# A hybrid decoder layer on one core: the first channel group's projections per token block over four weight tiles, and the input's squares added on VectorE

## The chip, the cores and the metric

The kernel runs on one core of a Trainium2 chip. The metric is the device time of the whole launch in microseconds (us), as the median of several runs. Besides these, one execution was recorded by the hardware profiler; its rows are quoted below.

## What is computed

One layer on 2048 tokens of 1024 channels, in float32. The input is RMS-normalised and projected; the projection feeds two token mixers; their outputs go through one output projection; a squared-ReLU MLP follows. Phase A of the kernel, which the change is about, computes the lines up to the silu of `u`:

```python
h_in = rms_norm(x, pre_mix_norm_w)                 # x * rsqrt(mean(x*x) + EPS) * w
proj = jnp.einsum("bsd,de->bse", h_in, w_in)       # -> qk_raw, v, o, gates, conv_val, conv_gate
qk = silu(causal_depthwise_conv(qk_raw, qk_conv_w, qk_conv_b))        # width 4
u = conv_val * sigmoid(conv_gate)
u = causal_depthwise_conv(u, conv_w, conv_b)                          # width 31
y_conv = silu(layer_norm_per_group(u))                                # 4 groups of 128 channels
h_tilde = mlstm_chunkwise(q, k, v, i_pre, f_pre)                      # chunks of 128 tokens
y = concat([y_mlstm, y_conv]) @ w_out;  x = x + rms_norm(y)
x = x + rms_norm(relu(rms_norm(x) @ w_ff1)**2 @ w_ff2)
```

## The kernel before

**Phases.** Phase A makes the normalised input and all input projections and stores what the mixers need in DRAM. Phase B walks the 16 chunks of the mLSTM and makes the output projection. The MLP follows. Each float32 operand of a projection is split into a high and a low part, so every product of two tiles is three matmuls.

**Token blocks.** The 2048 tokens are four blocks (`tb`) of 512; a block has eight k-tiles (`kt`) of 128 channels. Per block: ScalarE squares the eight tiles (`square_x`, L378); GpSimd adds them in seven steps of 128x512 (L276) for blocks 1 to 3, while for block 0 TensorE itself sums the eight squares; a matmul with ones (`sum_squares`, L301, L305) sums over channels; ScalarE makes the reciprocal root in two activations (`rstd_x`, L386, L388); VectorE scales each tile (L558), ScalarE copies its high part (L394), VectorE subtracts for the low part (L553).

**Slots.** TensorE's work in phase A is a list of 100 slots, each one weight tile times one token block (24 matmuls of 128x512), or for `v` and `o` a pair of weight tiles times two chunks (48 of 128x256). Channel group g has the slots `gate` and `val` for each of the four blocks, then `qk` for two tiles j and four blocks. The order is group 0, group 1, eight `v` slots, group 2, eight `v`, group 3, four `gates`, sixteen `o`. Slot s writes PSUM bank s mod 6 and waits until slot s-6 has been evacuated: by VectorE for `val` (`glu`, L585, the gated product into `u_buf`), by ScalarE for all others. Every engine goes through `for s in range(N_SLOTS)` in program order, so one late instruction holds all that stand behind it on its engine. The matmul with ones for block tb+1 stands behind slots 0, 2 and 4.

**The wide convolution.** A unit u is one group and one half (1024 tokens), eight units in all. It has a first tap on ScalarE (`first_tap`, L445) and 30 taps on VectorE (`tap`, L597), each over 128x1024. `tap_plan()` fixes when it is built how many taps follow each slot: a slot gives room 100, a tap takes 26, half a qk convolution takes 78 (`convolve_qk`, L609: three steps of 128x1024). `CONV_END[u]` is the slot after whose taps unit u is complete. From it hang, by slots: +1 two sums by TensorE (which waits in its queue for tap 30(u+1)), +2 centring on VectorE (L635), +3 squaring on ScalarE, +4 again two sums by TensorE, +5 the reciprocal root on ScalarE (L501 to L506), +6 a multiply on GpSimd (L284), +7 silu and the store to `yc` on ScalarE (L510, L513). The code of the planner before gives `CONV_END` = 19, 28, 38, 46, 57, 65, 75, 85. A `u_buf` ring of three means that the `glu` that begins unit u waits for the taps of unit u-3, and the planner forces these to be placed before it.

**The end of phase A.** `TAIL_SLOT` is 94. ScalarE does the softplus of the gates in slot 94; behind slot 95 TensorE waits for the reciprocal root of all eight units, since these use the same PSUM banks, and then makes `carry_in`; `carry_out` and `columns` stand behind slots 96 and 97. GpSimd loads the gate rows and later stores the rows `neg_m` and `inter`. SyncE waits for every store of `qk` and `yc`, then loads chunks 0 and 1 (ten DMAs of 256 KB, L921 to L923) and their rows (four, L927). Phase B begins when chunk 0 is complete.

**Weights.** A weight tile is loaded into a ring of four, its high part made by ScalarE (L401), its low part by VectorE for tiles 0 to 3 (L568) and by GpSimd for the others (L259).

## Time and profile before

| what | value |
|---|---|
| median of 3 runs | 2191.96 us (2190.08 to 2196.56) |
| profiled execution, its own time | 2193.84 us |
| span of the profiled execution | 2192.0 us |
| TensorE, matmuls busy | 2108.2 us, 96% |
| VectorE busy | 1481.8 us, 68% |
| ScalarE busy | 892.9 us, 41% |
| GpSimd busy | 530.9 us, 24% |
| mean granted TensorE clock | 0.984 |

The span is from the first to the last instruction; 1.84 us of the profiled execution's time lie around it. The shares are averages over stages with different limits, so a stage is read from its own window. A matmul's busy time is that of one instruction, and neighbours overlap.

### The profile page before, as it was taken

To read this page: it belongs to the slowest core of one execution; us is meant where nothing else is said; L and a number is where in the kernel's file an instruction comes from. 1 tells how busy PE (TensorE), PEld (TensorE's weight loads), DVE (VectorE), ACT (ScalarE), POOL (GpSimd) and SP (SyncE) were. 2 spreads that over 40 slices of the span, in tenths; PEclk is the share of its full clock that TensorE was granted. 3 is DMA by queue.
4 is the path that set the end of the run, shared out by engine and by line. 5 is a ranking of instruction groups with operands and counts; after the bars stand their busy time and mean duration, and the time that the engine had idled before them with its cause. 6 is when DMAs were issued, how large, how long until landed. Compare 5 with 4: busy or idle time off the path is not lost. (4 is left out here: it accounts for less than half of the span.)

```text
span 2192.0 us, 27093 instructions
## 1 busy us (share of the span) xinstructions
PE 2108.2 (96%) x10177; PEld 1758.5 (80%) x10177; DVE 1481.8 (68%) x1922; ACT 892.9 (41%) x1504; POOL 530.9 (24%) x304
## 2 busy tenths in 40 slices
PE   5899999999998999979999989999999999999998
PEld 3588988987987888758888878888878888888886
DVE  6789999979336777776666776666745536544275
ACT  5432423324243544545454554444513313223153
POOL 4202102112110232143222232223172233500012
PEclk8999999999999999989999999999999999999999
DMA  5011212202264767554555655554666464543366
GB/s 193 20 58 39 83 44 66 80 20 71 66 227 152 237 229 244 182 177 156 159 159 159 217 181 159 159 159 155 222 248 232 154 246 149 198 173 135 135 240 211
DMA packets 253522, 339.19 MB, mean 155 GB/s; under 512 B 11537, under 2 KB 196113, under 8 KB 239569
## 3 DMA queue, kind: packets, MB, share of 16 engines
q1 hardware_dynamic: 219344, 316.29, 43.2%
q10 hardware_dynamic: 33728, 21.04, 3.1%
q8 instruction: 82, 1.34, 0.2%
q14 instruction: 48, 0.39, 0.1%
q0 software_dynamic: 320, 0.13, 0.0%
HBM read 226.14 MB, written 111.28 MB: 154 GB/s over the span
## 5 line engine op out<-in xcount | busy, mean ns | idle before, releaser
L1561 PE MATMUL psum<-x_hi,w_hi_P 128*128 128x512 f32 x896 | 353.2, 394 | 21.3 <-DVE x_lo L1508 21.3
L1561 PE MATMUL psum<-x_lo,w_hi_P 128*128 128x512 f32 x896 | 351.8, 393 | 0.0
L1561 PE MATMUL psum<-x_hi,w_lo_P 128*128 128x512 f32 x896 | 351.8, 393 | 0.0
L1763 PE MATMUL psum<-w_hi,hid_hi 128*128 128x512 f32 x896 | 348.7, 389 | 1.7 <-DVE hid_lo L1655 1.7
L597 DVE SCALAR_TENSOR_TENSOR c_buf<-u_buf,par_a,c_buf 128x1024 f32<-128x1024 f32 x240 | 342.8, 1430 | 8.5 <-ACT c_buf L445 1.3
L1763 PE MATMUL psum<-w_lo,hid_hi 128*128 128x512 f32 x896 | 348.6, 389 | 0.0
L1763 PE MATMUL psum<-w_hi,hid_lo 128*128 128x512 f32 x896 | 348.6, 389 | 0.0
L1655 DVE TENSOR_TENSOR hid_lo<-hid_raw,hid_hi 128x1024 fp32r<-128x1024 f32 x112 | 176.4, 1612 | 209.6 <-ACT hid_hi L1650 209.6
L1477 POOL TENSOR_TENSOR w_raw<-w_raw 128x512 f32<-128x512 f32 x128 | 181.8, 1442 | 406.0 <-DVE w_lo_P L1490 401.4
L1490 DVE TENSOR_TENSOR w_lo_P<-w_raw,w_hi_P 128x512 fp32r<-128x512 f32 x224 | 182.3, 826 | 107.9 <-ACT w_hi_P L1486 104.9
L1650 ACT ACTIVATE hid_hi<-hid_raw 128x1024 fp32r<-128x1024 f32 x112 | 112.9, 1051 | 348.7 <-DMA hid_raw<-scratch_hid 348.7
L1486 ACT ACTIVATE w_hi_P<-w_raw 128x512 fp32r<-128x512 f32 x224 | 137.0, 627 | 259.2 <-PE psum L1561 258.5
L1561 PEld LDWEIGHTS psum<-x_hi,w_hi_P 128*128 128x128 f32 x896 | 170.2, 190 | 60.7 <-issue 25.6
L1561 PEld LDWEIGHTS psum<-x_lo,w_hi_P 128*128 128x128 f32 x896 | 170.4, 190 | 35.5
L1561 PEld LDWEIGHTS psum<-x_hi,w_lo_P 128*128 128x128 f32 x896 | 170.2, 190 | 35.7
L1763 PEld LDWEIGHTS psum<-w_hi,hid_hi 128*128 128x128 f32 x896 | 168.2, 188 | 37.4 <-issue 2.5
L1763 PEld LDWEIGHTS psum<-w_hi,hid_lo 128*128 128x128 f32 x896 | 168.2, 188 | 34.9
L1763 PEld LDWEIGHTS psum<-w_lo,hid_hi 128*128 128x128 f32 x896 | 168.2, 188 | 34.8
L1611 POOL TENSOR_TENSOR w_raw<-w_raw,w_grain 128x1024 f32<-128x1024 f32 x48 | 139.1, 2912 | 224.9 <-DMA w_grain<-in_w 224.9
L259 POOL TENSOR_TENSOR w_lo<-w_raw,w_hi 128x1024 fp32r<-128x1024 f32 x21 | 56.8, 2715 | 332.6 <-ACT w_hi L401 332.6
L337 PE MATMUL psum<-big_hi,w_hi 128*128 128x512 f32 x272 | 114.4, 420 | 15.2 <-DVE big_lo L553 11.6
L337 PE MATMUL psum<-h_hi,w_hi 128*128 128x512 f32 x272 | 109.5, 402 | 7.2 <-ACT h_hi L394 4.0
(231 smaller groups left out, 3885.0 us busy)
## 6 DMA issues: line engine op xcount, KB each, us to landing
scratch_hid<-stage SPq DMA_DIRECT2D x224, 256.0 KB, 3.7
hid_raw<-scratch_hid SPq DMA_DIRECT2D x56, 1024.0 KB, 4.9
w_raw<-in_w SPq DMA_DIRECT2D x52, 1024.0 KB, 5.1
w_grain<-in_w SPq DMA_DIRECT2D x48, 512.0 KB, 5.1
x_raw<-scratch_h2s SPq DMA_DIRECT2D x14, 1024.0 KB, 7.6
w_raw<-in_w_in SPq DMA_DIRECT2D x25, 512.0 KB, 3.9
scratch_h2s<-h2s SPq DMA_DIRECT2D x8, 1280.0 KB, 9.3
scratch_qk<-qout ACTq DMA_DIRECT2D x16, 512.0 KB, 3.0
```

Of the source, the lines that this page charges most:

```text
L259: nc.gpsimd.tensor_tensor(w_lo[:, RING[t]], w_raw[:, RING[t]], w_hi[:, RING[t]].bitcast(F32), ALU.subtract).then_inc(sem["w_lo"], 1)
L337: mm = nc.tensor.matmul(out, a, b, start=kt == 0 and i == 0, stop=kt == KT - 1 and i == 2)
L597: nc.vector.scalar_tensor_tensor(out=out, in0=src, scalar=par[:, CONV_W + g * CW + k:CONV_W + g * CW + k + 1], in1=out, op0=ALU.mult, op1= ...
L1477: nc.gpsimd.tensor_tensor(raw_1(op), raw_1(a), raw_1(b), ALU.subtract).then_inc(sem["w1_t"], 1)
L1486: nc.scalar.activation(w1_hi[op][:], raw_1(op), ACT.Copy).then_inc(sem["w1_hi"], 1)
L1490: nc.vector.tensor_tensor(w1_lo[op][:], raw_1(op), w1_hi[op][:].bitcast(F32), ALU.subtract).then_inc(sem["w1_lo"], 1)
L1561: mm = nc.tensor.matmul(psum[:, bank_1(op, g), :], l, r, start=kt == 0 and i == 0, stop=kt == 3 and i == 2)
L1611: nc.gpsimd.tensor_tensor(part, part, grain[:, n % 2], alu).then_inc(sem["w2_t"], 1)
L1650: nc.scalar.activation(hid_hi[n % HID_RING][:, half_fps(h)], hid_raw[n % HID_RING][:, half_fps(h)], ACT.Copy).then_inc(sem["hid_hi"], 1)
L1655: nc.vector.tensor_tensor(hid_lo[n % HID_RING][:, half_fps(h)], hid_raw[n % HID_RING][:, half_fps(h)], hid_hi[n % HID_RING][:, half_fps(h) ...
L1763: mm = nc.tensor.matmul(psum[:, bank, :], l, r, start=f == 0 and k == 0, stop=f == NFP - 1 and k == 2)
```

## The change

Group 0 now runs block by block: slots 4tb to 4tb+3 are `qk` 0, `qk` 1, `gate` 0, `val` 0 of block tb, so all four first weight tiles are in use from the start. Tiles 2 and 3 are loaded ahead of blocks 2 and 3 of the input and are split behind block 0's normalisation. ScalarE's squares of a block fill all eight quarters of `c_buf` and of a part of `u_buf`, and VectorE adds them in three steps, 128x2048, 128x1024 and 128x512 (`add_squares`), behind the previous block's normalisation. Of block 0 VectorE makes the last four squares. The matmul with ones stands inside slots 2, 6 and 10, behind k-tile 3, 3 and 2. The evacuations of slots 0 to 9 are spread between the blocks. The half convolutions of `qk` 0 and 1 are placed at slots 13, 15, 17 and 19, in a second buffer for j = 1, and the planner gives room for taps only behind slot 13. Evaluated with the new lines, it gives 4 taps behind slot 15, then 1, 3, 1, 3, and 18 behind slot 20 (forced by the ring of `u_buf`), none behind 21 to 24, and `CONV_END` = 20, 36, 44, 54, 63, 71, 82, 90. GpSimd loads the gate rows in slot 90, and the rows have addresses of their own.

```diff
 def group_slots(g):
+    if g == 0:
+        for tb in range(NTB):
+            out += [("qk", 0, tb), ("qk", 1, tb), ("gate", 0, tb), ("val", 0, tb)]
+        return out
...
+def glu_end(u):
+
+    return SLOTS.index(("val", u // 2, 2 * (u % 2) + 1))
+
+
+FIRST_LOOP = 13
+Q_AT = {(j, half): {(0, 0): 13, (0, 1): 15, (1, 0): 17, (1, 1): 19}.get((j, half)) or SLOTS.index(("qk", j, 2 * half + 1))
+        for j in range(8) for half in range(2)}
+EARLY_EVACS = 10
+X_SUMS = {(2, 3): 1, (6, 3): 2, (10, 2): 3}
+
+
+def convs_at(s):
+    return [q for q in Q_AT if Q_AT[q] == s]
...
-        ready = DVE_TAPS * sum(SLOTS.index(("val", u // 2, 2 * (u % 2) + 1)) <= s for u in range(N_UNITS))
-        if s >= 2 * NTB:
-            room += 100 - 13 * (SLOTS[s][0] == "val")
-        if s and SLOTS[s - 1][0] == "qk" and SLOTS[s - 1][2] % 2 == 1:
-            room -= 78
+        ready = DVE_TAPS * sum(glu_end(u) <= s for u in range(N_UNITS))
+        if s > FIRST_LOOP:
+            room += 100 - 13 * (SLOTS[s][0] == "val") - 78 * len(convs_at(s - 1))
         more = max(0, min(ready - n, room // 26))
...
-FIRST_TAP = [max(min(s for s in range(N_SLOTS) if TAPS[s] > DVE_TAPS * u) - 1, glu_slot(u) + 2) for u in range(N_UNITS)]
+FIRST_TAP = [max(min(s for s in range(N_SLOTS) if TAPS[s] > DVE_TAPS * u) - 1, glu_end(u)) for u in range(N_UNITS)]
...
         def x_sq(n):
 
-            return c_buf[:, n % 4 // 2, n % 2 * TB:(n % 2 + 1) * TB]
-
-        def x_adds(n):
-
-            return (KT - 1) * (n // KT - 1) + max(n % KT, 1)
+            n %= KT
+            buf = c_buf[:, n // 2] if n < KT // 2 else u_buf[:, n // 2 - 1]
+            return buf[:, n % 2 * TB:(n % 2 + 1) * TB]
+
+        def x_squares(n):
+
+            return n + 1 - (KT // 2 if n >= KT // 2 else 0)
+
+        def x_total(tb):
+            return qout[:, (tb % 2) * TB:(tb % 2 + 1) * TB]
+
+        def qk_raw(j, half):
+            return qraw[:, half] if j != 1 else qraw_1[:, half]
...
             load_x(0)
             load_w(0)
             load_w(1)
-            for tb in range(1, NTB):
-                load_x(tb)
+            load_x(1)
             load_w(2)
             load_w(3)
+            for tb in range(2, NTB):
+                load_x(tb)
...
-            for tb in range(1, NTB):
-
-                total = qout[:, (tb % 2) * TB:(tb % 2 + 1) * TB]
-                for kt in range(1, KT):
-                    n = KT * tb + kt
-                    pool.wait_ge(sem["x_sq"], n + 1)
-                    if kt == 1:
-                        if tb == 3:
-                            pool.wait_ge(sem["x_sum"], KT + 1)
-                        a = x_sq(n - 1)
-                    else:
-                        pool.wait_ge(sem["x_add"], x_adds(n - 1))
-                        a = total
-                    nc.gpsimd.tensor_tensor(total, a, x_sq(n), ALU.add).then_inc(sem["x_add"], 1)
             tail["masks"](pool)
...
+                if s == TAIL_SLOT - 4:
+                    tail["load_gates"](pool)
...
-            for b in range(2):
-                pool.wait_ge(sem["c_out"][b], 16 * (N_UNITS // 2))
-            pool.wait_ge(sem["q_out"], 16 * 16)
-            tail["load_gates"](pool)
+            tail["store_rows"](pool)
...
                 if tb == 0:
                     for kt in range(KT):
-                        pe.wait_ge(sem["x_sq"], kt + 1)
+                        if kt < KT // 2:
+                            pe.wait_ge(sem["x_sq"], x_squares(kt))
+                        else:
+                            pe.wait_ge(sem["x_sq_dve"], kt - KT // 2 + 1)
                         nc.tensor.matmul(psum[:, 6, :], ones[:], x_sq(kt), start=kt == 0,
                                          stop=kt == KT - 1).then_inc(sem["x_sum"], 1)
                 else:
-                    pe.wait_ge(sem["x_add"], x_adds(KT * tb + KT - 1))
-                    nc.tensor.matmul(psum[:, 6 + tb % 2, :], ones[:], qout[:, (tb % 2) * TB:(tb % 2 + 1) * TB],
-                                     start=True, stop=True).then_inc(sem["x_sum"], 1)
+                    pe.wait_ge(sem["x_add"], 3 * tb)
+                    nc.tensor.matmul(psum[:, 6 + tb % 2, :], ones[:], x_total(tb), start=True, stop=True).then_inc(sem["x_sum"], 1)
...
+                        if (s, kt) in X_SUMS:
+                            sum_squares(X_SUMS[(s, kt)])
...
-                if s in (0, 2, 4):
-                    sum_squares(1 + s // 2)
...
-                act.wait_ge(sem["evac"]["act"], evacs(s, "act"))
-                act.wait_ge(sem["q_head"], 1)
+            def first_tap_qk(j, half):
+
+                act.wait_ge(sem["evac"]["act"], evacs(SLOTS.index(("qk", j, 2 * half + 1)), "act"))
+                act.wait_ge(sem["q_head"], 2)
...
-            for n in range(KT):
+            for n in range(KT // 2):
                 square_x(n)
             split_w(0)
             split_w(1)
...
                 rstd_x(tb)
                 if tb == NTB - 1:
                     nc.scalar.preload_act_table_set(SILU_TANH)
-                    evacuate(0)
+                    evacuate(9)
                 for kt in range(KT):
                     high_x(KT * tb + kt)
-            split_w(2)
-            split_w(3)
+                if tb == 0:
+                    split_w(2)
+                    split_w(3)
+                    evacuate(0)
+                    evacuate(1)
+                if tb in (1, 2):
+                    nc.scalar.preload_act_table_set(SILU_TANH)
+                    for s in {1: (2, 4, 5), 2: (6, 8)}[tb]:
+                        evacuate(s)
+                    nc.scalar.preload_act_table_set(LN_EXP)
             for s in range(N_SLOTS):
                 for t in tiles_split_at(s):
                     if t >= 4:
                         split_w(t)
-                if s >= 1:
+                if s >= EARLY_EVACS:
                     evacuate(s)
                 for u in units_at(s, AT_SQUARE):
...
+            def square_x(n):
+
+                dve.wait_ge(sem["x_in"][n // (KT // 2)], 16)
+                nc.vector.tensor_tensor(x_sq(n), x_at(0, n), x_at(0, n), ALU.mult).then_inc(sem["x_sq_dve"], 1)
+
+            def add_squares(tb):
+
+                dve.wait_ge(sem["x_sq"], x_squares(KT * tb + KT - 1))
+                four, two = c_buf[:], c_buf[:, 0]
+                nc.vector.tensor_tensor(four, four, u_buf[:, 1:3, 0:HALF], ALU.add).then_inc(sem["x_add"], 1)
+                dve.wait_ge(sem["x_add"], 3 * tb - 2)
+                nc.vector.tensor_tensor(two, two, c_buf[:, 1], ALU.add).then_inc(sem["x_add"], 1)
+                dve.wait_ge(sem["x_add"], 3 * tb - 1)
+                if tb == 3:
+                    dve.wait_ge(sem["x_sum"], KT + 1)
+                nc.vector.tensor_tensor(x_total(tb), two[:, 0:TB], two[:, TB:HALF], ALU.add).then_inc(sem["x_add"], 1)
...
+            for n in range(KT // 2, KT):
+                square_x(n)
             split_w(0)
             split_w(1)
             for tb in range(NTB):
                 normalise_x(tb)
-            split_w(2)
-            split_w(3)
+                if tb + 1 < NTB:
+                    add_squares(tb + 1)
+                if tb == 0:
+                    split_w(2)
+                    split_w(3)
+                if tb == 1:
+                    glu(3)
+                if tb == 2:
+                    glu(7)
             for s in range(N_SLOTS):
-                if SLOTS[s][0] == "val" and s > 1:
+                if SLOTS[s][0] == "val" and s >= EARLY_EVACS:
                     glu(s)
-                if s == 0:
-                    nc.vector.memset(qraw[:, 0, 0:QW - 1], 0.0).then_inc(sem["q_head"], 1)
                 for n in range(TAPS[s - 1] if s else 0, TAPS[s]):
                     tap(n)
-                if s >= 1 and SLOTS[s - 1][0] == "qk" and SLOTS[s - 1][2] % 2 == 1:
-                    convolve_qk(s - 1)
+                for j, half in convs_at(s - 1):
+                    convolve_qk(j, half)
...
+ROWS_AT = 215904
...
+        def store_rows(pool):
             pool.wait_ge(sem["rows_done"], 2)
```

## Rows read from the trace of the kernel before

**Rows 1.** Windows of the first 97 us: busy time of each engine, granted TensorE clock, DMA.

```profile
22.20:97.00 74.80, 56.13 (x173) 36.30 (x174) 59.93 (x64) 37.66 (x64) 33.82 (x25) 0.79 0.11 42
```

**Rows 2.** Timeline: first projection matmul; ScalarE's evacuations as slots 8 and 15 end.

```profile
22.19 0.47 PE L337 MATMUL psum<-big_hi,w_hi 128*128 128x512 f32 x1 [3.71 <-DVE big_lo L553]
...
108.45 0.60 ACT L415 ACTIVATE qraw<-psum 128x512 f32<-128x512 f32 x1 [6.97 <-PE psum L337]
...
146.53 0.60 ACT L415 ACTIVATE qraw<-psum 128x512 f32<-128x512 f32 x1 [3.38 <-PE psum L337]
```

**Rows 3.** Timeline of VectorE: start, duration; a normalise step under GpSimd, two without.

```profile
48.22 1.77 DVE L558 SCALAR_TENSOR_TENSOR big_raw<-big_raw,par_a,rstd_a 128x512 f32<-128x512 f32 x1
...
93.04 0.75 DVE L558 SCALAR_TENSOR_TENSOR x_raw<-x_raw,par_a,rstd_a 128x512 f32<-128x512 f32 x1
...
94.31 0.75 DVE L558 SCALAR_TENSOR_TENSOR x_raw<-x_raw,par_a,rstd_a 128x512 f32<-128x512 f32 x1
```

**Rows 4.** Timeline: a wide subtraction, the ones matmul, the reciprocal root, the normalise steps.

```profile
16.84 2.36 DVE L568 TENSOR_TENSOR w_lo<-w_raw,w_hi 128x1024 fp32r<-128x1024 f32 x2 [13.81 <-ACT w_hi L401]
...
40.26 1.05 PE L305 MATMUL psum<-qout,ones 128*128 128x512 f32 x2
...
41.35 0.69 ACT L386 ACTIVATE rstd_a<-psum,eps 128x512 f32<-128x512 f32 x1 [3.76 <-PE psum L305]
...
42.73 1.42 DVE L558 SCALAR_TENSOR_TENSOR big_raw<-big_raw,par_a,rstd_a 128x512 f32<-128x512 f32 x2 [4.03 <-ACT rstd_a L388]
...
82.95 0.69 ACT L386 ACTIVATE rstd_a<-psum,eps 128x512 f32<-128x512 f32 x1 [3.35 <-PE psum L305]
```

**Rows 5.** Windows around a gap of TensorE: busy times, then the granted clock.

```profile
18.50:22.20 3.70, 0.01 (x1) 0.04 (x1) 2.96 (x5) 2.82 (x5) 0.00 (x0) 1.00 1.05 386
...
24.50:35.60 11.10, 5.83 (x11) 3.33 (x12) 11.10 (x8) 4.87 (x9) 8.71 (x6) 0.50 0.54 202
35.60:40.20 4.60, 4.56 (x11) 2.87 (x10) 3.01 (x4) 1.88 (x4) 3.29 (x2) 0.50 0.00 0
40.20:42.00 1.80, 1.80 (x7) 1.12 (x6) 0.00 (x0) 0.65 (x1) 0.00 (x0) 0.97 0.00 0
```

**Rows 6.** Timeline: taps alone, half convolutions alone and beside a GpSimd split.

```profile
103.62 10.53 DVE L597 SCALAR_TENSOR_TENSOR c_buf<-u_buf,par_a,c_buf 128x1024 f32<-128x1024 f32 x8
115.71 3.93 DVE L609 SCALAR_TENSOR_TENSOR qout<-qraw,par_a,qout 128x1024 f32<-128x1024 f32 x3 [1.57 <-ACT qout L459]
...
131.32 5.95 DVE L609 SCALAR_TENSOR_TENSOR qout<-qraw,par_a,qout 128x1024 f32<-128x1024 f32 x3 [2.93 <-ACT qout L459]
...
132.32 2.55 POOL L259 TENSOR_TENSOR w_lo<-w_raw,w_hi 128x1024 fp32r<-128x1024 f32 x1 [8.96 <-ACT w_hi L401]
```

**Rows 7.** Timeline of VectorE: the gated product of slot 21.

```profile
180.94 0.69 DVE L585 SCALAR_TENSOR_TENSOR u_buf<-th,psum 128x512 f32<-128x512 f32 x1 [0.70 <-PE psum L337]
```

**Rows 8.** Window from slot 21 to the last tap; TensorE's wait for that tap.

```profile
181.00:567.00 386.00, 382.93 (x2069) 326.11 (x2067) 363.64 (x266) 132.42 (x145) 64.96 (x23) 1.00 0.20 62
...
566.96 1.12 PE L341 MATMUL psum<-c_buf,ones 128*128 128x512 f32 x2 [1.97 <-DVE c_buf L597]
```

**Rows 9.** Timeline of ScalarE: end of slot 90, then unit 7's reciprocal root.

```profile
593.72 0.60 ACT L428 ACTIVATE th<-psum 128x512 f32<-128x512 f32 x1 [6.88 <-PE psum L327]
...
597.18 1.06 ACT L505 ACTIVATE rstd_a<-rstd_a 128x1024 f32<-128x1024 f32 x1
```

**Rows 10.** Timeline and one window from unit 7's store to the first chunk.

```profile
605.24 0.60 ACT L428 ACTIVATE th<-psum 128x512 f32<-128x512 f32 x1 [5.08 <-PE psum L327]
...
611.56 0.72 POOL L760 DMA_DIRECT2D gi<-scratch_gates  x1 [10.83 <-DMA scratch_yc<-c_buf]
...
629.02 0.45 SPq L921 DMA_DIRECT2D q_t<-scratch_qk  x1
...
640.00:642.00 2.00, 2.00 (x19) 2.00 (x18) 2.00 (x3) 1.09 (x2) 0.00 (x0) 1.00 1.08 397
...
647.32 0.60 ACT L428 ACTIVATE th<-psum 128x512 f32<-128x512 f32 x1 [1.40 <-PE psum L327]
...
649.05 2.22 DVE L887 SCALAR_TENSOR_TENSOR p_c<-negm_b,cols,mask 128x128 f32<-128x128 f32 x4 [1.50 <-DMA winter_b<-scratch_rows]
```

69 lines of the change are left out of this document (31 added, 38 removed).

## The prediction

> **What bounds the kernel now.** I read the windows of the first 97 us first, since the change starts there. TensorE shows 56.1 of 74.8 us busy at a mean granted clock of 0.79 [rows 1]. The timeline gives the loss: the first projection matmul starts at 22.2, slot 8 ends at 108.4 and slot 15 at 146.5 [rows 2]. That is 5.44 us a slot at full speed, so sixteen slots and three matmuls with ones (0.85 each) are 89.6 us, and 34.7 of the 124.3 are lost waiting for normalised tiles or running at half clock. Then I read the rest of phase A. From slot 21 to the last tap, TensorE is busy 382.9 of 386 us and VectorE 363.6, with only 22.4 us idle [rows 8]. So VectorE is nearly a second bound, and behind slot 86 TensorE already waits 1.97 us for a tap [rows 8]. Last I read the hand-over to phase B: slot 99 ends at 647.3 and the first chunk is complete at 649.05, when its last row DMA lands [rows 10]. What lies behind moves with that point.
>
> **The front: 30.5 us less.** Gone are 21 GpSimd adds. Under one of them a VectorE step takes 1.77 us against 0.75, and without them two steps and one tile come every 1.27 us [rows 3]. So block 0's last tile is ready at about 30.5 (22.2 and seven times 1.27, less the scaling that no longer follows), slot 0 ends at 31 and slot 1 at 36.5. Added are three VectorE steps a block over 2048, 1024 and 512 elements. Two subtractions of 1024 take 2.36 [rows 4], which makes 2.3 + 1.2 + 0.65 = 4.1 us. Behind block 0 they run from 30.5 to 34.6, the split of tile 2 to 35.9, and slot 2 wants it at 36.5. The cover is 0.6 us; if it goes, the lateness is paid in full. The four squares of block 0 on VectorE cost nothing, since the ones matmuls of that block are back to back. The ones matmul of the next block starts 2.7 us into slot 4tb+2. ScalarE's root starts 1.1 later and the scaling 1.4 after that [rows 4], and eight tiles take 10.4. The last tile is thus ready 15.6 us into slot 4tb+2, and TensorE reaches it at 11.7 + 4.8 = 16.5. From slot 1 on nothing waits, and slot 15 ends at 36.5 + 14 x 5.44 + 2.6 = 115.3. For block 3, ScalarE's table load and evacuation come first. I take 116, with bounds 115 and 119 (the upper if slots 0 and 1 run at half clock). Before, it was 146.5.
>
> **The wait for unit 0: 18.4 us given back.** TensorE stands behind slot 21 until tap 30. In the new order VectorE starts those taps only behind the gated product of slot 15, at 116. Thirty taps at 1.31 are 39.3; the halves (0,1) and (1,0) placed among them 3.93 each, 7.9; three gated products 1.8 [rows 6, 7]. One GpSimd split falls beneath: beside such a split of 2.55 us a half took 5.95 instead of 3.93, so 2.0 [rows 6]. The sum is 51.0, so tap 30 ends at 167.0. TensorE is there at 116 + 6 x 5.44 = 148.6. Queued behind the waiting sums are slots 22 and on, and VectorE, once it has caught up, waits for `val` slot 23. Bounds: 16.5 (no lock, short steps) to 20.5 (late first taps on ScalarE). VectorE's 8 us of idle before 116 can't help, as the code holds the taps.
>
> **The clock: 2.3 us.** After a gap of 3.7 us and thin work TensorE ran at 0.50, and dense work from 35.6 on needed 4.6 us until it had 1.0 back at 40.2 [rows 5]. After 18 us idle I count 4.6 us at half speed, 2.3 lost; bounds 0 and 3.
>
> **The middle: 2.1 us.** Behind slot 25 the plan has 31 taps done where the old one had 55, so until unit 7 ends VectorE does 24 more, 31.4 us, in five more slots. I followed VectorE's queue slot by slot: 1.31 a tap, 3.86 a half, 0.62 a gated product, 1.14 a centring, 1.9 for each GpSimd operation beneath, waits for `val` slots and first taps as the code has them. For the old order it puts the last tap's end at 567.6 (measured 566.9) and TensorE's waits for taps at 1.9 us (measured 3.1 of idle [rows 8]). For the new order, the waits are 4.0: 0.3 behind slot 45, 2.1 behind 72, 1.6 behind 83. Unit 7's last tap ends 3.7 us before TensorE asks for it behind slot 91. The difference is 2.1. Bounds: -3 (no wait left) and +5 (GpSimd's operations cost more, below).
>
> **The end of phase A: 4.5 and 2.3.** Unit 7 now ends at slot 90, so its reciprocal root falls in ScalarE's slot 95. There it comes behind the evacuation, and TensorE needs it behind that same slot, for `carry_in`. From the evacuation's start to the end of the root took 593.72 to 598.24, 4.5 us [rows 9]. Before it fell in slot 90, with five slots to spare. The gap is longer than the 3.7 us one, after which the clock fell [rows 5], so another 2.3; the 1.97 us wait left it at full [rows 8]. Bounds: 4.3 to 7.
>
> **The start of phase B: 3.8.** Unit 7's silu and store now stand in slot 97. The store had landed 6.3 us after the evacuation ahead of it started, 605.24 to 611.56 [rows 10]. SyncE waits for it, so the ten chunk loads, which were issued from 629.0, ahead of slot 97's end, begin about when slot 98 ends, 5.8 us before slot 99's end. Fourteen loads of 256 KB and two stores are 4.2 MB, at the 397 GB/s of that stretch [rows 10] 10.6 us, and a microsecond to start. Less the two rows of chunk 1, the first chunk is complete about 5.5 us after slot 99, against 1.75 before. Bounds: 0 and 4.5. The weights of the output projection are ahead of it and cost nothing.
>
> **The sum.** -30.5 + 18.4 + 2.3 + 2.1 + 4.5 + 2.3 + 3.8 = +2.9 us. The span goes from 2192.0 to 2194.9. The profiled execution's own time was 2193.84, 1.84 around the span; the median 2191.96 is as good as the span, so I forecast 2194.9.
>
> **Rivals.**
> First, the gain survives at the end. If the clock stays up at both gaps and the first chunk's loads land as early as before, 8.4 us go: 2186.5; if the 4.0 us of tap waits go too, 2182.5. For it speak that the DMA queues and ScalarE have room there, and that one gap of 1.97 us left the clock at full. Against it, SyncE's wait and slot 95's queue are in the code. It decides for faster from 9.5 us below my sum on. 0.22.
> Second, VectorE falls further behind. Beside a GpSimd split of 2.55 us it lost 2.0 [rows 6]. If each operation beneath costs VectorE 2.4 instead of 1.9, the walk gives 10.1 us of tap waits for the new order and 5.4 for the old, and a wait for unit 0 longer by 0.5: together 3.1 us more, 2198. Against it, the walk of the old order would then end slot 91 at 603.7 and its last tap at 571.1, and that tap ended at 566.9. 0.13. The Trainium skill, "SBUF — State Buffer", section "Who interferes with whom", has the loser of the shared port pair blocked for the whole instruction, which would be this case.
> Third, the front is not as dense. The root of each next block now hangs on TensorE's place inside slot 4tb+2. If each block loses 3 us to a late split or sum, slot 15 ends at 125, and all behind it comes 9 us later, since the taps wait for slot 15: 2204. The cover is 0.6 to 0.9 us a block. 0.12.
> Fourth, the change does not do what it says: the adds are gone, but the blocks keep the old pace. VectorE's steps would have to stay at 1.77, and block 3, with no adds beside it, ran at 1.27 a tile [rows 3]; the old end of slot 15 and the other parts would give 2194.9 + 30.5 = 2225.4. 0.02.
>
> **How the numbers follow.** My forecast has 0.51, from 2188 to 2200 by its own bounds. The whole range is 2184 to 2204: most of the first rival, the second, and the third up to its price. About 0.3%, 6.6 us, is what a measurement of this kernel can tell from no change. Faster by more: the first rival's larger part and a little of mine, 0.20. Slower by more, above 2198.5: the third and fourth, half of the second and the upper edge of mine, 0.25. Same: 0.55.
>
> **What the changed profile would show.** Right: the ends of slots 0, 1 and 15 near 31, 36.5 and 116; VectorE's steps at 0.75 throughout; a TensorE wait of about 18 us for a tap behind slot 21, the clock at 0.50 after it; waits of a few us at 72 and 83; a wait of 4.5 for ScalarE's root behind slot 95; chunk loads issued only near slot 98's end, and the first chunk 5 to 6 us behind slot 99. Wrong: slot 15 past 119, no wait behind 21, a tap wait behind 91, or SyncE issuing at the old place.

## The result, and the profile after

The changed kernel took 2207.1 us (median of 5 runs, 2204.38 to 2209.72), against 2191.8 before (5 runs, 2190.08 to 2196.56). The ratio is 1.0065, with a 95% interval of 1.0054 to 1.0077, so the change costs time. The profiled execution's own time is 2204.82 and its span 2203.0, against 2193.84 and 2192.0: 11.0 us more in this pair, where I had forecast 2.9. The medians are 15.3 apart. The account below is made in the profiled pair, and a wait's number in square brackets stands behind the instruction that waited.

The front came as forecast. First the windows: the first 97 us, the stretch of the wait for unit 0, the whole of [rows 8], two stretches with a gap in them, and phase B's start. The columns are the window, its length, the busy us (and number of instructions) of TensorE's matmuls, its weight loads, VectorE, ScalarE and GpSimd, then the granted clock, the DMA share and GB/s.

```profile
22.20:97.00 74.80, 74.33 (x310) 58.94 (x310) 54.03 (x75) 46.95 (x75) 0.00 (x0) 0.97 0.12 43
150.00:200.00 50.00, 33.48 (x131) 25.53 (x132) 24.87 (x22) 11.20 (x12) 4.11 (x2) 0.80 0.10 32
181.00:567.00 386.00, 376.55 (x2040) 320.43 (x2039) 346.00 (x259) 125.50 (x139) 62.51 (x22) 0.99 0.19 60
500.00:550.00 50.00, 43.22 (x196) 34.73 (x195) 48.90 (x34) 20.06 (x23) 11.89 (x4) 0.93 0.21 65
624.00:628.00 4.00, 3.07 (x15) 2.85 (x16) 2.56 (x7) 3.44 (x3) 2.36 (x1) 0.57 1.06 402
656.00:664.00 8.00, 4.74 (x20) 4.39 (x21) 3.89 (x7) 3.32 (x7) 1.26 (x1) 0.50 0.81 277
```

TensorE is now busy 74.3 of the first 74.8 us at a clock of 0.97, where it was 56.1 at 0.79 [rows 1]. Then VectorE's timeline in the front: the three wide additions, the gated product of slot 15, the first taps of unit 0 and five of the later ones.

```profile
29.94 2.29 DVE L572 TENSOR_TENSOR c_buf<-c_buf,u_buf 128x2048 f32<-128x2048 f32 x1
32.26 1.23 DVE L574 TENSOR_TENSOR c_buf<-c_buf 128x1024 f32<-128x1024 f32 x1
33.52 0.69 DVE L578 TENSOR_TENSOR qout<-c_buf 128x512 f32<-128x512 f32 x1
...
115.45 0.69 DVE L616 SCALAR_TENSOR_TENSOR u_buf<-th,psum 128x512 f32<-128x512 f32 x1 [3.00 <-PE psum L352]
116.05 6.56 DVE L628 SCALAR_TENSOR_TENSOR c_buf<-u_buf,par_a,c_buf 128x1024 f32<-128x1024 f32 x5
...
138.77 6.56 DVE L628 SCALAR_TENSOR_TENSOR c_buf<-u_buf,par_a,c_buf 128x1024 f32<-128x1024 f32 x5
```

Slot 15 ends at 115.4 against 146.5 [rows 2], a gain of 31.1 (read at VectorE's gated product after, at ScalarE's evacuation before). But the first tap starts at 116.05, and before it started at 103.62 [rows 6]. TensorE is 31 us ahead and VectorE 12 us behind. TensorE's waits in the rest of phase A, from its timeline, with the first wait of phase B last:

```profile
166.52 3.78 PE L358 MATMUL psum<-c_buf,ones 128*128 128x512 f32 x4 [18.47 <-DVE c_buf L628]
...
471.78 1.98 PE L358 MATMUL psum<-c_buf,ones 128*128 128x512 f32 x4 [2.39 <-DVE c_buf L628]
...
542.20 3.78 PE L358 MATMUL psum<-c_buf,ones 128*128 128x512 f32 x4 [6.78 <-DVE c_buf L628]
...
624.93 0.26 PE L830 MATMUL psum<-ident,a_max 64*1 64x64 f32 x1 [4.62 <-ACT rstd_a L521]
...
657.82 2.04 PE L1062 MATMUL psum<-q_t,k_t 128*128 128x128 f32 x8 [6.71 <-DMA winter_b<-scratch_rows]
```

They stand behind slots 21, 72, 83, 95 and 99. The same four matmuls with ones take 1.98 us behind the 2.39 us wait and 3.78 behind the long ones, which is half clock. The account, read from slot 25 on at ScalarE's evacuations and VectorE's first state update (656.13 before, 666.73 after). The kernel before:

```profile
204.47 0.60 ACT L415 ACTIVATE qraw<-psum 128x512 f32<-128x512 f32 x1
...
622.51 0.60 ACT L428 ACTIVATE th<-psum 128x512 f32<-128x512 f32 x1 [0.71 <-PE psum L327]
...
656.13 1.13 DVE L1234 SCALAR_TENSOR_TENSOR state<-state,decay_b,psum 128x129 f32<-128x129 f32 x4 [0.21 <-PE psum L1042]
```

The changed kernel, from slots 0 and 1 on:

```profile
31.62 0.57 ACT L427 ACTIVATE qraw<-psum 128x512 f32<-128x512 f32 x1
36.59 0.60 ACT L427 ACTIVATE qraw<-psum 128x512 f32<-128x512 f32 x1 [4.39 <-PE psum L352]
...
194.08 0.60 ACT L427 ACTIVATE qraw<-psum 128x512 f32<-128x512 f32 x1 [5.48 <-PE psum L352]
...
620.35 0.60 ACT L440 ACTIVATE th<-psum 128x512 f32<-128x512 f32 x1 [2.42 <-PE psum L342]
...
651.14 0.60 ACT L440 ACTIVATE th<-psum 128x512 f32<-128x512 f32 x1 [0.72 <-PE psum L342]
...
666.73 1.12 DVE L1277 SCALAR_TENSOR_TENSOR state<-state,decay_b,psum 128x129 f32<-128x129 f32 x4 [1.82 <-PE psum L1085]
```

| part | forecast | measured |
|---|---|---|
| front, to slot 15 | -30.5 | -31.1 |
| wait for unit 0 and clock, to slot 25 (204.47 before, 194.08 after) | +20.7 | +20.7 |
| middle, to slot 95 (622.51 before, 620.35 after) | +2.1 | +8.2 |
| end of phase A, to slot 99 (647.32 before, 651.14 after) | +6.8 | +6.0 |
| start of phase B, to the first state update (+10.6 there) | +3.8 | +6.8 |
| the rest of the kernel | 0 | +0.4 |
| sum | +2.9 | +11.0 |

At slot 25, 10.4 us of the gain are left, at slot 95 2.2, and at slot 99 the changed kernel is 3.8 behind.

### The profile page after: what moved, and what is told of

Same layout as the page of the kernel before. It is cut to its first block and busy times, and to the rows that moved or that the text cites. A ratio compares the mean times of both kernels' runs of the same rounds, so it can differ in the third digit from the quotient of the medians.

```text
span 2203.0 us, 27060 instructions
## 1 busy us (share of the span) xinstructions
PE 2104.8 (96%) x10177; PEld 1761.7 (80%) x10177; DVE 1475.5 (67%) x1936; ACT 894.7 (41%) x1504; POOL 500.5 (23%) x283
## 5 line engine op out<-in xcount | busy, mean ns | idle before, releaser
L628 DVE SCALAR_TENSOR_TENSOR c_buf<-u_buf,par_a,c_buf 128x1024 f32<-128x1024 f32 x240 | 334.5, 1396 | 13.9 <-ACT c_buf L457 6.5
L1910 DVE TENSOR_TENSOR c<-c,psum 128x512 f32<-128x512 f32 x96 | 65.5, 683 | 71.9 <-PE psum L1604 71.8
```

The costliest lines, as they stand in the source:

```text
L628: nc.vector.scalar_tensor_tensor(out=out, in0=src, scalar=par[:, CONV_W + g * CW + k:CONV_W + g * CW + k + 1], in1=out, op0=ALU.mult, op1= ...
L1910: nc.vector.tensor_tensor(out[:], a[:], ps1(op, g), ALU.add).then_inc(sem["gather"], 1)
```

## The experiments

Each is timed beside runs of the kernel before on the same chip, and its ratio is to that kernel. The changed kernel's own is 1.0065.

**1. Unit 0's LayerNorm steps three slots later.**

```diff
-    return [u for u in range(N_UNITS) if CONV_END[u] + step == s]
+    return [u for u in range(N_UNITS) if CONV_END[u] + (3 if u == 0 else 0) + step == s]
```

> The changed kernel with the six LayerNorm steps of unit 0 (from its group sum on TensorE on) three slots later, behind slot 24 and not behind slot 21; taps, gates and projections keep their order. Theory (the wait behind slot 21 and the half clock after it are the 20.7 us that the trace of the changed kernel lost between slots 15 and 25, and nothing else on the way needs unit 0 so early): TensorE runs slots 21 to 24 without a wait, slot 25 is read at 173 to 176 us (194.08 in the changed kernel), the last tap of unit 0 still ends near 166. If all of it survived to the end the profiled execution would take 2184; VectorE's list is unchanged, so I expect that later taps are late against the faster TensorE and that waits behind slots 37, 45, 72 and 83 give back some 5 us: 2184 to 2192, ratio to the kernel before 0.997 to 1.001. Rival (VectorE is the bound of the whole middle): TensorE only runs ahead and stops behind slot 37 or 45 for the taps of unit 1 or 2 by nearly the whole 20 us, and the time stays at 2203 to 2206, ratio 1.0055 to 1.007. Second rival: the three late taps' successors hold a PSUM bank, and TensorE waits at slot 27 for the read of slot 21 (it comes only behind the 18 taps, near 167): slot 27 begins near 182 without a wait, so this one asks for less than 0 us and is expected not to show.

Measured: 2188.63 us, ratio 0.9977 (0.9968 to 0.9987). Its TensorE waits:

```profile
167.82 2.77 PE L358 MATMUL psum<-c_buf,ones 128*128 128x512 f32 x4 [2.15 <-DVE c_buf L628]
...
456.15 1.98 PE L358 MATMUL psum<-c_buf,ones 128*128 128x512 f32 x4 [2.40 <-DVE c_buf L628]
...
526.59 3.78 PE L358 MATMUL psum<-c_buf,ones 128*128 128x512 f32 x4 [6.82 <-DVE c_buf L628]
```

The last tap of unit 0 ends at 167.8 (166.5 in the changed kernel), and TensorE waits 2.15 us for it instead of 18.47. The waits behind 72 and 83 come 15.6 us sooner and are as long as in the changed kernel. So the theory holds in the main for this wait, though I had expected no wait at all there and 5 us lost again later. The rival that VectorE would take the 20 us back at the next unit falls. VectorE's instructions were not done any faster: it only waited less for TensorE, and its last tap starts at 571.8, not 587.6. The span fell by 12.7 us and the median by 18.5 (11 runs, of which the profiled one was the longest); that difference belongs to what stays open below.

**2. The last unit one slot earlier.**

```diff
+        cost = 26 if s < 82 else 24
-        more = max(0, min(ready - n, room // 26))
+        more = max(0, min(ready - n, room // cost))
```

> The changed kernel with the taps of the last unit planned a little denser from slot 82 on (24 hundredths of a slot for each, not 26), so that they end with slot 89 and not 90 and its six LayerNorm steps move up by one slot; its root then stands ahead of the softplus, in slot 94. Theory (the end of phase A and the start of phase B are late because of this one step): the wait of TensorE's transposes behind slot 95 for the root (4.62 us) and the half clock after it go, slot 99 is read 5 to 6 us sooner against slot 93 than now; the last store of yc goes out one slot earlier, the first chunk is complete 1 to 3 us behind slot 99 and not 6.7, TensorE starts the scores with its clock up. Gain 6 (end) plus 3 to 6 (start), less up to 2 for a wait for the last tap behind slot 90 (taps ended 0.8 us behind that slot): time 2194 to 2199, ratio 1.001 to 1.004. Rival (the start of phase B is set by the rows and by the landing of seven loads for each chunk, not by the store): only the 6 us come back and the first chunk is again 5 us or more behind slot 99: 2199 to 2200, ratio 1.004. Rival two: VectorE has no room for it, the wait behind slot 90 takes 4 us or more, and nothing is gained.

Measured: 2205.21 us, ratio 1.0057 (1.0044 to 1.0069). The root left slot 95, and the wait stayed:

```profile
626.74 0.26 PE L831 MATMUL psum<-ident,a_max 64*1 64x64 f32 x1 [4.51 <-DVE a_max L881]
```

The releaser has changed from ScalarE's root to VectorE's running maximum. The root now runs ahead of the softplus on ScalarE and pushes it, and the maximum comes from the softplus. My theory took one of two chains through the same engine for the only one. Neither rival is what happened: nothing was gained, but no wait of 4 us stood behind slot 90.

**3. Tiles 21 and 22 loaded ahead of tile 20.**

```diff
-            for t in range(4, N_TILES):
+            for t in list(range(4, 20)) + [21, 22, 20] + list(range(23, N_TILES)):
```

> The changed kernel with the weight loads of tiles 21 and 22 issued ahead of that of tile 20 on SP's queue: they need only slots 70 and 71 to be done, but stand behind tile 20, which waits for slot 75, so that three loads of 512 KB go out together at 490.2 us, 1.7 us ahead of the store of a qk half. Theory (that collision made the store land after 7.0 us and not 2.9, held the next first tap of qk and with it VectorE for 6.61 us, and so made the 6.78 us wait behind slot 83 and the half clock after it): the store lands after 4.5 us or less, VectorE's idle stretch there is 3 us or less, the wait behind slot 83 shrinks by 3 to 4 us to about 3, and the end comes 4 to 6 us sooner: 2199 to 2201, ratio 1.004 to 1.005. Rival (VectorE is late by its own work, and the store only moved where it stood): the wait behind slot 83 stays at 5 us or more, ratio 1.006 to 1.007. A third possibility is that what is gained there is lost again at the root in slot 95, as TensorE arrives earlier and ACT does not: the wait behind slot 95 would grow by what that behind 83 shrinks.

Measured: 2201.08 us, ratio 1.0035 (1.0023 to 1.0048). ScalarE's timeline of the changed kernel, from the store's issue, and then that of this one:

```profile
491.84 0.37 ACTq L478 DMA_DIRECT2D scratch_qk<-qout  x1
498.98 1.15 ACT L469 ACTIVATE qout<-qraw,par_a 128x1024 f32<-128x1024 f32 x1 [7.17 <-DMA scratch_qk<-qout]
```

```profile
492.12 0.37 ACTq L478 DMA_DIRECT2D scratch_qk<-qout  x1
495.60 1.15 ACT L469 ACTIVATE qout<-qraw,par_a 128x1024 f32<-128x1024 f32 x1 [3.52 <-DMA scratch_qk<-qout]
```

With one weight load beside it the 512 KB store held ScalarE 3.52 us, with three 7.17. VectorE's idle stretch behind it fell from 6.61 to 2.94, and TensorE's wait behind slot 83 from 6.78 to 3.11. The first scores begin 2.7 us sooner and the span is 3.3 shorter. The theory holds: 3.7 us of the middle's loss were a collision of transfers that the new order had made. The kernel before issues the same three loads, from 499.33 on, but its silu and store follow 3.9 us later (503.19) and not 1.7, and there the store held ScalarE 3.88 us.

**4. The wide additions on GpSimd.**

```diff
-                nc.vector.tensor_tensor(four, four, u_buf[:, 1:3, 0:HALF], ALU.add).then_inc(sem["x_add"], 1)
+                nc.gpsimd.tensor_tensor(four, four, u_buf[:, 1:3, 0:HALF], ALU.add).then_inc(sem["x_add"], 1)
```

(and the same for the other two additions, in GpSimd's list ahead of its masks)

> The changed kernel with the three wide additions of a token block's squares on GpSimd, as they stand, instead of on VectorE (4.2 us a block there). Estimate from rows of both traces: GpSimd took 2.47 us for a 128x1024 operation and 1.54 for a 128x512 one, so 4.9 + 2.5 + 1.5 = 8.9 us a block. Theory (VectorE's adds are on the path from one token block to the next, and it matters which engine does them): every block's root is 4.7 us later less VectorE's own glu and splits that stood behind them (0.7 to 2.4), the front ends 10 to 12 us later (slot 15 read at 125 to 127, 115.4 in the changed kernel), and this passes through to the end, as VectorE starts unit 0's taps as much later: ratio 1.011 to 1.012. Rival (the new order alone made the gain, the adds have room): slot 15 within 3 us of 115.4 and the ratio 1.006 to 1.008.

Measured: 2207.13 us, ratio 1.0067 (1.0053 to 1.0081). The same three additions took 4.23, 2.68 and 1.58 us on GpSimd (means of three blocks), 8.5 a block where I had estimated 8.9, and yet slot 14's evacuation came only 1.3 us later (111.30 against 110.01). The theory was wrong: in the changed kernel VectorE stood idle 5.08 and 7.34 us ahead of the next two blocks' scaling, and the slower additions fell into that gap, though only just: TensorE waited 0.46 us for the first block's, and VectorE's two splits beside them took 7.76 us instead of 2.35.

```profile
30.48 4.25 POOL L288 TENSOR_TENSOR c_buf<-c_buf,u_buf 128x2048 f32<-128x2048 f32 x1 [29.53 <-ACT u_buf L404]
31.38 7.76 DVE L600 TENSOR_TENSOR w_lo<-w_raw,w_hi 128x1024 fp32r<-128x1024 f32 x2 [0.78 <-ACT w_hi L426]
...
40.33 1.12 PE L334 MATMUL psum<-qout,ones 128*128 128x512 f32 x2 [0.46 <-POOL qout L294]
```

The rival holds: which engine adds makes no difference to the time that these runs could tell. That TensorE's place for the sum's matmul sets the pace of the blocks fits with this, but no run moved it.

**5. The squares' half of the change alone.** The slot order of before, with the eight buffers, the shared squares and the wide additions.

```diff
 # the kernel before, with the new square_x, add_squares and x_sq
+X_SUMS = {(1, 5): 1, (3, 5): 2, (5, 5): 3}
...
+                        if (s, kt) in X_SUMS:
+                            sum_squares(X_SUMS[(s, kt)])
...
-                if s in (0, 2, 4):
-                    sum_squares(1 + s // 2)
```

> The kernel before, its slot order kept, with only the other half of the change: the squares of the first token block shared by ScalarE and VectorE, eight buffers for the squares, the three wide additions a block on VectorE, and the sum's matmul in the middle of slots 1, 3 and 5. Theory (the front's gain is the slot order's: TensorE has four slots of work for each token block and not two, and who adds is worth next to nothing, as GpSimd's wide additions had shown): slot 15 within 4 us of the 146.5 of before, ratio 0.998 to 1.002. Rival (the additions on VectorE, and VectorE's steps at 0.75 us without a busy GpSimd beside them, give a third of the 31 us by themselves): slot 15 near 136, ratio 0.995 or less.

Measured: 2182.86 us, ratio 0.9962 (0.9947 to 0.9977), faster than both kernels. ScalarE's evacuation of slot 15 and TensorE's waits:

```profile
134.17 0.60 ACT L408 ACTIVATE qraw<-psum 128x512 f32<-128x512 f32 x1 [3.48 <-PE psum L333]
```

```profile
493.46 1.98 PE L339 MATMUL psum<-c_buf,ones 128*128 128x512 f32 x4 [1.11 <-DVE c_buf L607]
...
554.50 1.98 PE L339 MATMUL psum<-c_buf,ones 128*128 128x512 f32 x4 [1.90 <-DVE c_buf L607]
...
636.28 1.13 PE L1033 MATMUL psum<-q_t,k_t 128*128 128x128 f32 x8 [1.45 <-DMA winter_b<-scratch_rows]
```

Slot 15 ends 12.4 us sooner than in [rows 2], and the first tap starts 12.4 sooner, at 91.3. Each of the three waits is within 0.4 us of that of the kernel before, and the span is 12.1 shorter (the medians 9.4). My theory was wrong and the rival right on the front; the ratio is a little above the 0.995 it asked for. A gain in the front that moves VectorE's first tap by the same amount comes through nearly whole. The other 18.7 us of the front's gain belong to the rest of the change, the slot order, and they come with a first tap 24.8 us later than here (116.1 against 91.3).

**6. Root and softplus one slot earlier.** Experiment 2, and besides:

```diff
-                if s == TAIL_SLOT:
+                if s == TAIL_SLOT - 1:
                     nc.scalar.preload_act_table_set(LN_EXP)
                     tail["softplus"](act)
...
-                if s == TAIL_SLOT - 4:
+                if s == TAIL_SLOT - 5:
                     tail["load_gates"](pool)
```

> The changed kernel with the last unit's steps one slot earlier, as in the experiment on the last unit, and with the softplus of the gates in slot 93 and their load by GpSimd one slot earlier too. There the root had moved ahead of the softplus and pushed it, so that TensorE waited 4.51 us for the running maximum from VectorE instead. Theory (both chains, root and softplus, each need ScalarE ahead of slot 95's end, and together they fit): TensorE's wait behind slot 95 is below 0.5 us and its clock stays up, slot 99 is read 5 to 7 us sooner against slot 93, yc's last store one slot earlier, and the first chunk is complete 3 to 4 us behind slot 99: 2196 to 2198, ratio 1.002 to 1.003. Rival (the gain at the end of phase A is taken back at the start of phase B, where 14 loads of 256 KB have to go out after the store of yc): slot 99 sooner by 5 us or more, but the scores begin at most 2 us sooner than in the last-unit experiment, ratio 1.005 or more.

Measured: 2199.47 us, ratio 1.0036 (1.0023 to 1.0048). The wait behind slot 95 is gone, there is one of 0.90 behind slot 90, and the first scores begin at 652.23 instead of 657.82, after a wait of 6.49. Slot 99's end, which is where that wait begins, came 5.4 us sooner (645.7 against 651.1), so the end of phase A gave back nearly its 6 us. The start of phase B gave 0.2. The theory is right on the two chains and wrong on what follows: I had expected the first chunk 3 to 4 us behind slot 99 and 2196 to 2198 us. The rival had too little: the scores begin 6.0 us sooner than in experiment 2, not at most 2.

**7. The chunk loads in the order of their data.**

```diff
-            for b in range(2):
-                sp.wait_ge(sem["c_out"][b], 16 * (N_UNITS // 2))
+            sp.wait_ge(sem["tap"], DVE_TAPS * N_UNITS)
             load(0)
             load(1)
+            sp.wait_ge(sem["c_norm"], N_UNITS)
+            load_k(0)
+            load_k(1)
             sp.wait_ge(sem["rows_out"], 2 * H * 16)
             load_rows(0)
             load_rows(1)
+            for b in range(2):
+                sp.wait_ge(sem["c_out"][b], 16 * (N_UNITS // 2))
+            load_yc(0)
+            load_yc(1)
```

(`load` without k and yc for these two chunks)

> The changed kernel with the loads of the first two chunks put in the order in which their data are there: q, v and o first, k once the last norm is done, the rows once they are stored, and yc last, alone behind the store of the last unit. In the changed kernel all 14 stand behind that store. Theory (the 6.71 us wait of the scores behind slot 99 is that queue, and TensorE's restart at 0.50 of its clock comes with it): the wait is below 1 us, the clock stays up through the first chunk, the state update of the first chunk comes 7 to 9 us sooner (666.73 now), time 2198 to 2200, ratio 1.003 to 1.004. Rival (the scores wait for what VectorE and ScalarE have to do for the first chunk, and the DMA was only the last of them): the wait changes its releaser and stays above 3 us, ratio 1.005 or more.

Measured: 2199.6 us, ratio 1.0034 (1.0021 to 1.0046). The first scores:

```profile
653.57 1.13 PE L1076 MATMUL psum<-q_t,k_t 128*128 128x128 f32 x8 [2.26 <-DMA yc_c<-scratch_yc]
```

The wait is 2.26 us and the eight scores take 1.13 us, where they took 2.04 behind the wait of 6.71. The scores begin 4.25 sooner, the first state update 4.65 (662.08), the second 5.48 (677.03 against 682.51), and the span is 6.5 shorter. The theory is right in kind, and its ratio was met; but the wait is not below 1 us, and the state update moved less than the 7 to 9 us that I had given it, since the scores still wait, now for yc.

**8. All of it together.** Experiments 3, 6 and 7, with the steps of unit 0 four slots later and those of units 5 and 6 one.

```diff
+    return [u for u in range(N_UNITS) if CONV_END[u] + {0: 4, 5: 1, 6: 1}.get(u, 0) + step == s]
```

> All of it in one: the changed kernel with the LayerNorm steps of unit 0 four slots later and those of units 5 and 6 one slot later, the weight loads of tiles 21 and 22 ahead of tile 20, root and softplus one slot earlier, and the chunk loads in the order of their data. Theory (the gain of the front is there to be had, and what ate it were five waits at TensorE, each from the placing of a step and not from VectorE's or the DMA's total work): no wait of TensorE above 1 us between slot 15 and the scores; time 2207 less 19 for unit 0, 4 for the loads, 4 for units 5 and 6, 6 for the end of phase A and 8 for the start of phase B, which is 2166; I give 2164 to 2176, ratio 0.987 to 0.993. Rival (VectorE's lateness comes up at the next step, whichever is moved: it has 240 taps and 16 short convolutions to do in slots 14 to 90, which are now 25 us shorter): the taps of the last units are late by 5 to 15 us, with a wait behind slots 83 or 90, and the ratio is 0.994 to 0.998.

Measured: 2179.25 us, ratio 0.9939 (0.9926 to 0.9951).

```profile
244.48 1.98 PE L359 MATMUL psum<-c_buf,ones 128*128 128x512 f32 x4 [2.38 <-DVE c_buf L629]
...
568.28 2.07 PE L359 MATMUL psum<-c_buf,ones 128*128 128x512 f32 x2 [8.06 <-DVE c_buf L629]
...
632.78 2.05 PE L1077 MATMUL psum<-q_t,k_t 128*128 128x128 f32 x8 [4.61 <-DMA yc_c<-scratch_yc]
```

```profile
140.00:568.00 428.00, 416.88 (x2303) 357.29 (x2301) 401.90 (x298) 138.90 (x155) 72.57 (x27) 0.99 0.20 62
```

The rival is the truer one here, though the ratio came just below its 0.994; my 2164 to 2176 us were missed. Four of the five waits are gone, that of the scores is 4.61 us, and two have come up for taps: 2.38 us, and 8.06 behind slot 90. VectorE is busy 401.9 of the 428 us from 140 us to there (94%, as in [rows 8]). So it is now what TensorE waits for, and it began late, at 116.6. Even so the kernel is 13.0 us faster than the one before on the same chip, whose first tap starts 13.0 us earlier (103.62): the last tap ends at 568.3 against 567.0, but TensorE is by then at slot 90 and not at slot 86.

**9. Ten taps in VectorE's gaps of the front.** Experiments 3 and 7, unit 0's steps two slots later, those of units 3, 5 and 6 one, and:

```diff
+EARLY_TAPS = {0: 4, 12: 2, 13: 2, 14: 2}
...
+        more = max(0, min(ready - n, room // (27 if s < 40 else 26))) if s > FIRST_LOOP + 1 else EARLY_TAPS.get(s, 0)
...
                 if tb == 2:
                     glu(7)
+                    for n in range(TAPS[0]):
+                        tap(n)
```

(and ScalarE's first tap of unit 0 behind its evacuations of block 2)

> The changed kernel with ten taps of unit 0 given to VectorE in gaps in which it stood idle: four behind the gated product of slot 7 (idle 7.3 us there) and six ahead of the first qk convolution (idle 7.9 us), the tap plan moved up to match, the last unit's convolution ending with slot 88, the LayerNorm steps of unit 0 two slots and of units 3, 5 and 6 one slot later, and the weight and chunk loads in the order of the experiment that took all of it together. Root and softplus keep their slots but for the plan. Theory (VectorE's chain from the first tap to the last is what phase A waits for: about 460 us from first to last tap in every kernel so far, 103.6 to 565 before, 116 to 589 after, 117 to 566 with all placings cured; the change lost because it starts that chain 12.4 us later): the last tap ends 11 to 14 us sooner than in that kernel, at 552 to 556, its wait of 8.06 us behind slot 90 falls to 3 or less, the scores begin 10 us sooner, 2164 to 2171, ratio 0.987 to 0.990. Rival (the placings decide and VectorE has room; its taps only fill what time there is): the last tap is no sooner than 562, ratio 0.993 to 0.995.

Measured: 2170.91 us, ratio 0.9903 (0.9887 to 0.9919), 21.6 us under the 2192.55 of before on the same chip. VectorE's timeline, and TensorE's last two waits:

```profile
82.07 5.25 DVE L633 SCALAR_TENSOR_TENSOR c_buf<-u_buf,par_a,c_buf 128x1024 f32<-128x1024 f32 x4 [1.31 <-ACT c_buf L460]
...
99.53 9.90 DVE L633 SCALAR_TENSOR_TENSOR c_buf<-u_buf,par_a,c_buf 128x1024 f32<-128x1024 f32 x6
```

```profile
557.88 3.59 PE L361 MATMUL psum<-c_buf,ones 128*128 128x512 f32 x4 [4.60 <-DVE c_buf L633]
...
625.98 2.02 PE L1083 MATMUL psum<-q_t,k_t 128*128 128x128 f32 x8 [3.45 <-DMA yc_c<-scratch_yc]
```

The last tap ends at 557.9, 10.4 us sooner than in experiment 8, for ten taps of 1.31 started earlier, and the span is 9.5 us shorter. That is what a bound on VectorE asks for. The rival, an end no sooner than 562, falls. The time is within the forecast, at its slow edge; its parts were missed: the last tap was to end at 552 to 556, the wait to be 3 us or less (4.60), the scores to begin 10 us sooner (6.8). 2.0 us of that are the six taps at 99.53, which took 9.90 us, where six alone take 7.9. The run also places units 0 and 3, the root and the softplus otherwise than experiment 8, so the 9.5 us are not all shown to be the taps'.

**10. The old order with the rest.** Experiment 5 with the loads of 3 and 7.

```diff
 # experiment 5, and load_w and the chunk loads as in experiments 3 and 7
```

> The kernel before with the squares' half of the change (that alone gave 0.9962) and with the weight loads of tiles 21 and 22 ahead of tile 20 and the chunk loads in the order of their data. It asks how much of the gain of the other kernels is to be had without the new slot order. Theory (in the old order TensorE waits only 1.1, 1.9 and 1.5 us, so there is nothing more to take): the first chunk's wait falls from 1.45 us to below 0.5, the start of phase B is set by VectorE's p_c (2.54 us), 2181 to 2183, ratio 0.9950 to 0.9962. Rival (the loads as they are now collide with the rows' stores or with the output weights): slower than the squares alone, ratio 0.997 or more.

Measured: 2183.51 us, ratio 0.9956 (0.994 to 0.9972), the same as experiment 5 within the intervals. In the old order there was nothing for those loads to save; the first scores even wait 2.68 us for yc, where I had expected less than 0.5. So the new order is worth having, 0.9903 against 0.9956, but only with its taps and steps placed for it.

## Why the prediction was wrong

**The front, the wait for unit 0 and the clock after it** were right, each within a microsecond: slot 0 was read at 31.6 and slot 1 at 36.6 (forecast 31 and 36.5), slot 15 ended at 115.4 (116), VectorE's steps took 0.75, and wait and clock cost 20.7 (20.7). That the additions cost nothing on VectorE was right too. Experiment 4 shows that they had the idle stretch of 5 to 7 us ahead of each block to fall into, several times the 0.6 to 0.9 us of cover that I had counted in my third rival.

**The middle is the step that failed**: 2.1 us forecast with an upper bound of 5, and 8.2 measured. I had forecast 4.0 us of tap waits, 1.6 behind slot 83 among them; the trace has 9.5, 6.8 of them behind slot 83. Less the 3.1 of the kernel before, which my walk had put at 1.9, that is 6.4 us, and half clock behind the long wait makes up the rest. My walk moved VectorE's, ScalarE's and TensorE's work slot by slot but gave every store the landing of the trace before, 2.9 us. The shift changed which transfers meet. Three weight loads went out at 490.17, and the store of a qk half behind them at 491.84 held ScalarE for 7.17 us, with VectorE idle 6.61 behind it. Experiment 3 undid the meeting and took 3.67 us off the wait. The rest of that wait (3.11 against my 1.6) is the walk's own error. Half clock behind the wait was not in my sum for this place, as I had forecast no long wait there; its four matmuls took 3.78 us instead of 1.98.

**The end of phase A** was right in size (6.0 for 6.8) and in mechanism (a wait of 4.62 for the root, the clock at 0.57 after it). What I had missed is that the softplus is a second chain through ScalarE that ends nearly as late once the root stands ahead of it (a wait of 4.51 in experiment 2), so that moving the root alone would not have saved it.

**The start of phase B** came out 3.0 above my 3.8. The queue was as described: the loads were issued from 644.78, and the first chunk was complete 6.7 us behind slot 99's end. I had put 5.5 there. From the first issue to the first scores it took 13.0 us, where my sum of bytes and rate gave 11.3; each load landed 2.6 to 6.9 us after its issue. The other part, 1.9 us more from the scores to the state update, is a term that I had left out: TensorE restarted at 0.50 after 6.71 us of idle, with the clock in 656 to 664 at 0.50. I had counted the clock only behind gaps inside phase A. In experiment 7 the wait and the half clock go together.

**What stays open.** The medians are 4.3 us further apart than the profiled pair: the profiled execution of the kernel before lies 2.0 above its median, that of the changed kernel 2.3 below. The changed kernel's runs lie between 2204.4 and 2209.7, and I have a trace of one of them only. Neither the account nor an experiment says where the others lose more.

**The rivals.** The first (the gain survives) had the right two places and the wrong sign: the queues did not have room. The second (each GpSimd operation costs VectorE 2.4 us and not 1.9) falls by the traces of both kernels. In phase A of the changed kernel 19 of VectorE's 288 taps and short-convolution steps took 3.28 to 3.51 us and all others less than 1.4, so every loss lies at 2.0 to 2.2. Experiment 9 shows how one comes about (timelines of 105.06 to 105.5 and of 106.2 to 108.3):

```profile
104.81 1.28 DVE L633 SCALAR_TENSOR_TENSOR c_buf<-u_buf,par_a,c_buf 128x1024 f32<-128x1024 f32 x1
105.05 3.31 POOL L290 TENSOR_TENSOR w_lo<-w_raw,w_hi 128x1024 fp32r<-128x1024 f32 x1 [103.05 <-ACT w_hi L416]
...
106.13 3.31 DVE L633 SCALAR_TENSOR_TENSOR c_buf<-u_buf,par_a,c_buf 128x1024 f32<-128x1024 f32 x1
```

The split is issued while a tap runs that ends at 106.09, and ends itself at 108.36, 2.27 us later. The next tap, beside it, takes 3.31 us instead of 1.28 and so loses 2.03. The length of the split says nothing of the loss: 2.55 us long in [rows 6] and 3.31 here, each cost 2.0, for the longer one is issued earlier in the running step. By the Trainium skill, "SBUF — State Buffer", section "Who interferes with whom", a VectorE instruction with two SBUF inputs contends with a GpSimd instruction that reads SBUF, and the shared port pair is an exclusive lock. The trace agrees, if the split stood still until 106.09: the tap loses nearly all of the 2.27 us from there on. The third (the front is not as dense) and the fourth (the blocks keep the old pace) fall with slot 15 at 115.4 and steps of 0.75. None of the four names what experiments 5, 8 and 9 showed. VectorE's list from the first tap to the last (463 us before, 452 in experiment 8) is about as long as TensorE's way from slot 15 to the wait for that last tap (444 us there), and the change moved TensorE's end of the front by -31.1 us and VectorE's beginning by +12.4.

## What to carry to other kernels

Where a front is made denser for one engine, see what it does to the next engine's first instruction. Before counting a gain, write down for each engine that is busy over nine tenths of the stage behind it (VectorE: 363.6 of 386 us in [rows 8]) when its long list starts, before and after. Here the part of the change that moved both by 12 us came through nearly whole, and the part that moved them apart cost, as it was placed, more than it gave. It is no ceiling, though: experiment 8 starts the list 13.0 us later than the kernel before and is still 13.0 us faster.

Steps that were placed by slot number for one order have to be placed again for another: of five waits of TensorE, 2 to 18 us each, four went and the fifth fell from 6.7 to 4.6 us, by moving a step or a load by one to four slots or behind another. What is cured in one place can come up in the next, as the 8.06 us behind slot 90 did. And a shifted schedule changes which transfers meet, so the landing time of a store is not a constant that can be carried over.

## What the runs showed of the hardware

Where TensorE stood idle 4.6 us or more ahead of the four matmuls with ones, these ran at half clock each time, in 3.59 to 3.78 us. At 3.11 us of idle they took 2.95. Around 2.4 us it went either way: 1.98 in the changed kernel and in experiments 1, 2, 3, 6, 7 and 8 (waits of 2.38 to 2.40), but 3.68 behind a wait of 2.39 in experiment 4, and 2.77 behind 2.15 in experiment 1. So the same wait can have two prices, which I had not expected. The first eight scores of phase B took 1.13 us behind waits of 1.45 to 2.68 us in four kernels, and 2.02 to 2.05 behind waits of 3.45 to 7.46 in the other eight.

A store of 512 KB on ScalarE's queue held it 3.52 us with one load of 512 KB issued 1.7 us ahead of it on SyncE's queue, 3.88 with three issued from 3.9 us ahead on, and 7.17 with three issued from 1.7 us ahead on. In the last case the DMA share in 492 to 498 was 0.99.

A GpSimd operation over 128x1024 that meets VectorE's taps lengthens one of them from 1.28 to about 3.31 us, whatever its own length in the trace (2.39 to 3.39 us for the weight splits of the changed kernel).
